# A four-layer transformer pass: residual stream with features on the partitions, norms applied to the finished product tiles

## The reference

```
# first block, for l in 0, 1
x = x + mixer(rms_norm(x, ln_mix[l]))        # w_in, GQA attention and latent attention, 2 output norms, w_o
x = x + memory_attention(rms_norm(x, ln_mem[l]), rms_norm(mem, ln_mem_kv[l]))   # 256 memory rows, 4 heads
x = x + expert_choice_moe(rms_norm(x, ln_ffn[l]))       # 16 experts, 64 tokens each, chosen by top_k
x = rms_norm(x, ln_final)
# second block, for l in 0, 1
x = x + concat(gating, pooling, retention)(rms_norm_2(x, norm1_g[l]) @ w_in[l]) @ w_out[l]
x = x + (silu(conv(h @ w_up)_gate) * conv(h @ w_up)_val) @ w_down[l],  h = rms_norm_2(x, norm2_g[l])
x = rms_norm_2(x, final_g)
# both norms:  x * rsqrt(mean(x * x) + 1e-6) * g     over the 1024 features of a token
```

## Time and profile before

| what | value |
|---|---|
| median of 3 runs | 2554.78 us (2554.11 to 2557.25) |
| the profiled execution: its time | 2554.77 us |
| its span in the profile | 2552.6 us |
| PE, DVE, ACT, POOL busy | 94%, 50%, 36%, 6% |
| mean granted clock of PE | 0.981 of full |
| HBM traffic | 355.76 MB read, 2.10 MB written |

### The profile page before, as it was taken

How to read it: one execution, slowest core, us unless ns; L and a number is a source line. 1 busy time by engine, 2 the same in 40 slices (tenths; PEclk the granted TensorE clock), 3 DMA queues, 4 the chain that set the end, 5 groups by cost and what they waited for, 6 DMA issues and landing times.

```text
span 2552.6 us, 28851 instructions
## 1 busy us (share of the span) xinstructions
PE 2407.1 (94%) x11244; PEld 1717.4 (67%) x11244; DVE 1280.5 (50%) x2170; ACT 920.9 (36%) x1608; POOL 162.6 (6%) x190
## 2 busy tenths in 40 slices
PE   8899996999898999699988999999999999999998
PEld 7655864444575477454446777888887768788887
DVE  4765544333458645523334445666523444666632
ACT  4575542111337745311113224444323213444421
POOL 1301002000021100200001000000000000000000
PEclk9999998999999999899998999999999999999999
DMA  4100406999520023489992212233334212233331
GB/s 176 50 1 34 155 20 255 394 394 394 193 67 17 1 83 124 158 318 394 394 358 92 75 50 83 91 99 99 99 99 133 74 50 76 82 99 99 93 108 56
DMA packets 131830, 359.74 MB, mean 141 GB/s; under 512 B 10992, under 2 KB 12016, under 8 KB 131440
## 3 DMA queue, kind: packets, MB, share of 16 engines
q1 hardware_dynamic: 131408, 357.48, 39.5%
q10 hardware_dynamic: 288, 0.42, 0.1%
HBM read 355.76 MB, written 2.10 MB: 140 GB/s over the span
## 4 chain that ended last, share of the span: by engine, by line
PE 85%; DVE 8%; ACT 4%; POOL 1%; issue 1%; DMA 0%; SPq 0%; POOLq 0%; DVEq 0%; ACTq 0%
PE ps L970 11%; PE ps L972 11%; PE ps L971 11%; PE ps L1188 9%; PE ps L984 6%; PE ps L985 6%; PE ps L986 6%; PE ps L1210 4%; PE ps L1108 3%; PE ps L1081 3%; PE ps L1089 2%; PE ps L1268 1%; PE ps L1150 1%; PE ps L1151 1%; PE ps L958 1%
## 5 line engine op out<-in xcount | busy, mean ns | idle before, releaser
L1855 DVE TENSOR_TENSOR wlo<-stage,whi 128x1024 fp32r<-128x1024 f32 x268 | 327.8, 1226 | 438.1 <-ACT whi L1330 437.6
L970 PE MATMUL ps<-hTh,whi 128*128 128x512 f32 x1232 | 489.8, 398 | 7.7 <-DVE hTl L1814 7.7
L972 PE MATMUL ps<-hTh,wlo 128*128 128x512 f32 x1232 | 480.0, 390 | 0.0
L971 PE MATMUL ps<-hTl,whi 128*128 128x512 f32 x1232 | 479.7, 389 | 0.0
L1330 ACT ACTIVATE whi<-stage 128x1024 fp32r<-128x1024 f32 x268 | 281.3, 1053 | 238.7 <-PE ps L986 238.2
L970 PEld LDWEIGHTS ps<-hTh,whi 128*128 128x128 f32 x1232 | 231.4, 188 | 61.5 <-issue 14.2
L971 PEld LDWEIGHTS ps<-hTl,whi 128*128 128x128 f32 x1232 | 231.5, 188 | 51.0 <-issue 4.3
L972 PEld LDWEIGHTS ps<-hTh,wlo 128*128 128x128 f32 x1232 | 231.3, 188 | 48.9
L1814 DVE SCALAR_TENSOR_TENSOR t<-ps,vecs,t 128x511 f32<-128x511 f32 (+1 forms) x176 | 131.6, 748 | 42.2 <-ACT t L1303 39.1
L1971 DVE TENSOR_REDUCE st<-ps 128x1 f32<-128x512 f32 (+1 forms) x160 | 100.9, 631 | 73.3 <-PE ps L1081 70.2
L984 PE MATMUL ps<-whi,inh 128*128 128x512 f32 x352 | 136.9, 389 | 0.0
(11 more groups left out here) (293 smaller groups left out, 3731.8 us busy)
## 6 DMA issues: line engine op xcount, KB each, us to landing
stage<-in_wpk SPq DMA_DIRECT2D x268, 512.0 KB, 3.6
wt<-in_wg SPq DMA_DIRECT2D x48, 512.0 KB, 11.8
stage<-in_wd SPq DMA_DIRECT2D x48, 512.0 KB, 12.4
ws<-in_wu SPq DMA_DIRECT2D x44, 512.0 KB, 11.5
ws<-in_wg SPq DMA_DIRECT2D x40, 512.0 KB, 11.4
wt<-in_wu SPq DMA_DIRECT2D x40, 512.0 KB, 11.6
wq<-in_wd SPq DMA_DIRECT2D x28, 512.0 KB, 12.5
wt<-in_wd SPq DMA_DIRECT2D x24, 512.0 KB, 12.0
```

The costliest lines, as they stand in the source:

```text
L970: pe.matmul(o, h, ah, start=k == 0, stop=False)
L971: pe.matmul(o, h, al, start=False, stop=False)
L972: t = pe.matmul(o, lo, ah, start=False, stop=k == 7)
L1855: ve.tensor_tensor(M.wlo[i % NW][:, :], M.stage[i % NSTAGE][:, :], f(M.whi[i % NW][:, :]), ALU.subtract).then_inc(*S.wlo.mark(("w", i)))
```

## The change

The residual `x` is held with features on the partitions, [128, 8, 512 tokens], from the first transposes of the input (`x_turn`) to the last stage.

- `om` takes the place of `tm` for the products that add to x (but the last): a chunk's weights are stationary, the activations move, and out is [128 features, 512 tokens] in four banks. As many matmuls of the same size.
- Behind each added tile stands `prep`: ACT copies x times the gain into the stage's `hTh`, then squares x into `nsq`; DVE makes `hTl`; POOL adds the squares to `nacc`. No norm, no `feat` (but for the memory rows).
- `head` takes the first two chunks of mixer, mixer2 and ffn together, k by k (`fmk`), a third behind them; meanwhile `scale` sums `nacc` over the partitions on PE (`nstat`), makes the inverse roots, spreads them over rows (`nrows`) and turns them (`nturn`); ACT copies that to `R`, [128, 512].
- Behind each `fm` of a normed input DVE multiplies the PSUM tile in place by R (`rs`), and what read the tile and waited for PE waits for `rs`.
- `scatter` writes feature tiles. The router stage turns x back into rows by 32 transposes for each layer (`xtok`), scaled by ACT. The final norm of the first block is a product on DVE by its gain and `R0` (`lnf`), and the next stage's statistics take it in through a product on PE (`pstat`).
- The last stage turns x back (`xt`, 32 transposes) and ends as before.
- The parts of mixer2's output (`part`) go to buffers of their own (`y2h`, `y2l`) as soon as these are free, those of the mixers and of the memory attention too.

The core of the diff (layout of buffers, and further waits on `rs` like those shown, are left out):

```diff
-    def fm(self, src, N=512):
+    def fm(self, src, ns, N=512):
         i = self.chunk()
         u = self.take()
         self.do("fm", i, u, src, N)
         self.rel.add(i)
+        if ns is not None:
+            self.do("rs", ns, i, u, 128)
         return i, u
...
+    def om(self, src, K, h, out, before={}):
+        us = [self.take() for _ in range(4)]
+        for c in range(K // 2):
...
+            i = self.chunk()
+            for j in range(4):
...
+                last = c == K // 2 - 1
+                self.do("om", i, us[j], src, c, j, last, j == 3)
+                if last:
+                    out(4 * h + j, us[j], ("om", i, j))
+            self.rel.add(i)
+
+    def residual(self, ns):
+        def go(f, u, key):
+            self.do("add", (ns,), f, u, key)
             self.drop(u)
-            if h == 1 and ahead:
-                self.norm_ahead(ns, m)
+            self.do("prep", ns, f)
         return go
...
+    def scale(self, ns, between=lambda: None):
+        if ns != 6:
+            u = self.take()
+            self.do("nstat", ns, u)
+            self.drop(u)
+        else:
+            self.do("nstat6", self.u6)
+            self.drop(self.u6)
+        self.do("nrows", ns)
+        between()
+        for part in ((0, 1) if ns == 6 else (0,)):
+            u = self.take()
+            self.do("nturn", ns, u, part)
+            self.drop(u)
+
+    def head(self, ns, s):
+        two = [(self.chunk(), self.take()) for _ in range(2)]
+        if ns == 6:
+            self.u6 = self.take()
+        for k in range(8):
+            for i, u in two:
+                self.do("fmk", i, u, s, k)
+            if ns == 6:
+                self.do("pstat", k, self.u6)
+        self.rel |= {two[0][0], two[1][0]}
+
+        def third():
+            two.append(self.fm(s, None))
+        self.scale(ns, third)
+        for i, u in two:
+            self.do("rs", ns, i, u, 128)
+        return two
...
@@ mixer
-        self.feat(s, NT)
+        ready = self.head(ns, s)
...
-        self.tm(("y", l), 8, NT, self.residual(3 * l + 1, 0), {(0, 1): self.tick, 1: self.tick, (1, 2): self.tick, 3: more})
+        self.om(("y", l), 8, 0, self.residual(3 * l + 1), {(0, 1): self.tick, 1: self.tick, (1, 2): self.tick, 3: more})
         self.feat(("memkv", l), 2)
-        self.tm(("y", l), 8, NT, self.residual(3 * l + 1, 1))
+        self.om(("y", l), 8, 1, self.residual(3 * l + 1))
...
@@ mixer2
+        if l == 0:
+            self.do("lnf")
...
@@ ffn
-        self.feat(s, NT)
+        ready = self.head(ns, s)
+
+        def first():
+            return ready.pop(0) if ready else self.fm(s, ns)
         for j in range(22):
-            i, u = self.fm(s)
+            i, u = first()
             self.do("conv", l, j, 0, u, i)
...
+        for m in range(NT):
+            for half in range(2):
+                u = self.take()
+                self.do("xt", m, half, u)
+                self.drop(u)
...
@@ whole
         self.do("start2")
-        for m in range(NT):
-            self.do("norm", 0, m)
+        us = [self.take() for _ in range(8)]
+        self.do("x_turn", us)
+        for f, u in enumerate(us):
+            self.do("x_copy", f, u)
+            self.drop(u)
+            self.do("prep", 0, f)
         for _ in range(2):
             self.do_split()
...
@@ act_program
+        elif name == "prep":
+            ns, k = a
+            src = SRC[ns]
+            q.wait_ge(*S.dve.at("x", ns, k))
+            copy(M.acts[src][k][0], M.x[:, k, :], ("hi", src, k), scale=gain(M, *src, k))
+            if k > 1:
+                q.wait_ge(*(S.pe if ns == 6 else S.pool).at("nacc", ns, k - 2 if ns == 6 else max(k - 2, 1)))
+            copy(M.nsq[k % 2][:, :], M.x[:, k, :], ("nsq", ns, k), f=ACT.Square)
...
@@ act_program, conv (and every other reader of a normed product)
-            q.wait_ge(*S.pe.at("fm", i))
+            q.wait_ge(*S.dve.at("rs", i))
...
@@ dve_program
+        elif name == "prep":
+            ns, k = a
+            src = SRC[ns]
+            hi, lo = M.acts[src][k]
+            q.wait_ge(*S.act.at("hi", src, k))
+            q.wait_ge(*S.dve.at("x", ns, k))
+            stt(lo, M.x[:, k, :], gain(M, *src, k), f(hi), ALU.mult, ALU.subtract, ("lo", src, k))
+        elif name == "rs":
+            ns, i, u, rows = a
+            b = M.ps[u[0]][0:rows, :]
+            q.wait_ge(*S.pe.at("fm", i))
+            q.wait_ge(*S.act.at("R", ns, 0))
+            tt(b, b, M.R[ns][0:rows, :], ALU.mult, ("rs", i))
```

More of the change, by code:

```diff
@@ L650, in mixer2, with last, first @@
             self.drop(u)
-            if n == 5:
-                self.do("point", "hdone2", l)
-                self.hdone = True
-                for p in range(4):
-                    part(p)
-            self.tick()
-        for p in range(4, 8):
-            if self.yf[p] and not self.yt[p]:
-                part(p)
-        self.tm(("y2", l), 8, NT, self.residual(7 + 2 * l, 0), {1: self.tick, 2: self.tick, 3: self.flush})
+            parts()
+            self.tick()
+        parts()
+        def last():
+            self.flush()
+            parts()
+        self.om(("y2", l), 8, 0, self.residual(7 + 2 * l), {1: self.tick, 2: self.tick, 3: last})
         assert not self.later and all(self.yt)
-        self.tm(("y2", l), 8, NT, self.residual(7 + 2 * l, 1))
+        self.om(("y2", l), 8, 1, self.residual(7 + 2 * l))
     def ffn(self, l):
         s = ("ffn", l)
+        ns = 7 + 2 * l
         self.do("point", "ffn", l)
-        self.feat(s, NT)
+        ready = self.head(ns, s)
+        def first():
+            return ready.pop(0) if ready else self.fm(s, ns)
         for j in range(22):
-            i, u = self.fm(s)
+            i, u = first()
             self.do("conv", l, j, 0, u, i)
             self.drop(u)
-            i, u = self.fm(s)
+            i, u = first()
             self.do("conv", l, j, 1, u, i)
@@ L973, in pe_program @@
             t.then_inc(*S.pe.mark(("w", i), ("fm", i)))
+        elif name == "om":
+            i, u, src, c, j, last, lastj = a
+            q.wait_ge(*S.whi.at("w", i))
+            q.wait_ge(*S.wlo.at("w", i))
+            if c == 0:
+                claim(u)
+            o = M.ps[u[0]][:, :]
+            for kk in range(2):
+                r = slice(kk * 512 + 128 * j, kk * 512 + 128 * j + 128)
+                h, lo = M.whi[i % NW][:, r], M.wlo[i % NW][:, r]
+                ah, al = operand(src, 2 * c + kk)
+                pe.matmul(o, h, ah, start=c == 0 and kk == 0, stop=False)
+                pe.matmul(o, lo, ah, start=False, stop=False)
+                t = pe.matmul(o, h, al, start=False, stop=last and kk == 1)
+            if last and lastj:
+                t.then_inc(*S.pe.mark(("om", i, j), ("w", i)))
+            elif last:
+                t.then_inc(*S.pe.mark(("om", i, j)))
+            elif lastj:
+                t.then_inc(*S.pe.mark(("w", i)))
         elif name == "tm":
@@ L1141, in pe_program @@
             t.then_inc(*S.pe.mark(("cum_turn", l)))
+        elif name == "xtok":
+            l, m, half, u = a
+            o = claim(u)
+            for i in range(4):
+                f_ = 4 * half + i
+                q.wait_ge(*S.dve.at("x", 3 * l + 2, f_))
+                t = pe.transpose(o[:, i * 128:(i + 1) * 128], M.x[:, f_, m * 128:(m + 1) * 128], M.ident)
+            t.then_inc(*S.pe.mark(("xtok", l, m, half)))
+        elif name == "xt":
+            m, half, u = a
+            o = claim(u)
+            for i in range(4):
+                q.wait_ge(*S.dve.at("x", 9, 4 * half + i))
+                t = pe.transpose(o[:, i * 128:(i + 1) * 128], M.x[:, 4 * half + i, m * 128:(m + 1) * 128], M.ident)
+            t.then_inc(*S.pe.mark(("xt", m, half)))
         elif name == "gather":
@@ L1428, in act_program @@
             if kind == "mem":
[L1429 to L1430 removed]
+                q.wait_ge(*S.pe.at("point", "memory", l))
+                copy(M.moh[:, p, :], M.ps[u[0]][:, :], ("hi", ("mo", l), p))
                 continue
```

468 lines of the change are left out of this document (283 added, 185 removed).

## The result

The changed kernel takes 2697.3 us (median of 4 runs, 2695.25 to 2699.38), the kernel before 2554.72 on the same chip: a ratio of 1.0556, 95% interval 1.0538 to 1.0574, slower by 142.6 us. The forecast was 2653 with a range of 2612 to 2700: the sign and the main mechanism hold, 44 us of the size don't. The result lies only 2.7 us inside the upper end, and just outside the narrower 2622 to 2696 that the prediction calls its own.

The account below looks back on a forecast made before the run. PE, busy 94% of the span, was taken to bound the kernel. Terms of +91.9, -6.9, -8.3, 0, +6.0 and +16 sum to +98.7 us on the 2554.78 us median: 2653 us, range 2612 to 2700.

Parts of the forecast that it names:

- The ring: Feed-forward: DVE and ACT wait for each other through rs, 13.01 us a step where PE needs 10.88; +91.9 us together.
- Rival A: Feed-forward: rs is hidden, as DVE's busy time with it stays under the span; 2554 us, no change; chance 0.06.
- rival B: Whole kernel: gaps and transposes go, the start hides, nothing new waits; -37.5 us, 2517 us; chance 0.06.
- The sign of what was to be seen: Feed-forward profile: PE waits for DVE wlo of some 43 us in each stage, no other PE wait that large.
- the start: Start of the kernel: prep of all eight tiles stands before the splits 0 and 1; +16 us, first fm at 28.
- the memory stages: Both layers: feat's banks come free later, the new scale chain is 0.8 shorter; +3.4 us each, +2.7 to the router's lgT.
- mixer 1: Mixer of layer 1: some 5 us gained, lost again by stat(cq) behind nturn, 0; a copy 0.7 us later.
- mixer2 of layer 0: Stage after scatter: tiles come 2.05 us apart, both first chunks done at 1354.3 where before 1366.3; -8.3 us.
- rival C: Feed-forward: PE idles 2.1 of 13 us and the granted clock falls; +190 us, 2845 us; chance 0.03.
- leaves 1.0: Feed-forward: the prediction would be wrong if the granted clock there leaves 1.0.
- The step on feat's banks: Memory stages: four banks are freed only by adds that alternate with hTl; second half of om starts 4.2 us later.
- rival D: Start and scatter stages: tiles contend with GpSimd and lose 10 us more; 2663 us; chance within the forecast's 0.82.

Follow-up runs that it names:

- e1: The changed kernel without the product by R in the two feed-forward stages, conv waiting for PE's fm again: 2598.9 us.
- e3: The kernel before, with a DVE product by a tile of ones behind each of the 88 feed-forward fm chunks, conv waiting for it: 2640.6 us.
- e8: The changed kernel with the feed-forward product by R cut to one column, its place in the queue and waits kept: 2650.7 us.
- e4: The changed kernel with the splits of weight chunks 0 and 1 put ahead of x_turn in the list: 2685.6 us.
- e6: The changed kernel with prep of the first four tiles of om(y) put behind feat of the memory rows: 2683.1 us.
- e5: The changed kernel with each add or x_copy put one tile ahead of prep on DVE: 2676.0 us.
- e12: The kernel of e5 with six of GpSimd's seven adds of squares a stage cut to one column: 2671.2 us.

## Why the prediction was right, and where its size failed

**The ring.** Right in place, price and form: 13.05 us for 13.01, 43.1 for 41.2 us in layer 0. rs was taken at 0.68 and has 0.69 (694 ns). The prediction says that no row shows a DVE product written back to PSUM, and puts its range between 422 and 1219 ns. Its rows don't, but the trace of the kernel before does, at the very price:

```profile
L1811 DVE TENSOR_TENSOR ps<-ps,xb 128x512 f32<-128x512 f32 x4 | 2.8, 692 | 0.1
```

e1 removes the ring, e3 brings it into the kernel before, e8 splits it. Rival A (rs hidden under idle time) is what the busy shares suggest, and e3 refutes it by itself; rival B fell with it. The sign of what was to be seen was right, its label not: I expected PE's waits under wlo, 43 us a stage. They stand under "issue", 54.3 us in all: one wait of 1.47 us in a step, of the 2.17 that it loses; the rest of each is drawn as busy matmuls. The number to read was the distance of the steps. The up projection of layer 0 takes 286 us, for 284 forecast.

**The size.** The spans miss the forecast by 46 us, and no error is offset by another: every stretch came out above its figure, the start by 11, the memory stages by 7.7 and 7.2, mixer 1 by 4.1, mixer2 by 7.6 and 2.0, the feed-forward by 1.9 and 3.8. A slip in the sum is small beside this: -12.0 + 2.9 + 1.1 for mixer2 of layer 0 is -8.0, not -8.3.

**The clock (rival C).** In the feed-forward it is 0.99: it lies at the lower level for 3.4 us from 1666.0, behind one wait of 3.24 us for wlo, and is full through all the ring's steps from 1684 to 1918. So C is out there, though by the letter ("leaves 1.0") the prediction's sign of being wrong appeared. Elsewhere the clock falls more: the window of the first products after, and of the first ones before (the earlier trace rows is its first row):

```profile
32.00:48.00 16.00, 15.26 (x61) 12.55 (x62) 3.07 (x4) 3.01 (x4) 0.66 (x1) 0.82 0.29 99
```

```profile
16.00:32.00 16.00, 14.94 (x66) 12.42 (x67) 8.95 (x12) 9.07 (x15) 0.00 (x0) 1.00 0.52 188
```

In the kernel after PE has stood 20 us, and then runs at the lower of its two levels (1.2 GHz) before it goes back to 2.4. The timeline shows it in the distance of the matmuls:

```profile
32.74 0.77 PE L1059 MATMUL ps<-hTh,whi 128*128 128x512 f32 x1 [20.28 <-DVE wlo L2077]
...
36.71 0.63 PE L1059 MATMUL ps<-hTh,whi 128*128 128x512 f32 x1
37.14 0.63 PE L1060 MATMUL ps<-hTh,wlo 128*128 128x512 f32 x1
...
39.31 0.39 PE L1059 MATMUL ps<-hTh,whi 128*128 128x512 f32 x1
39.54 0.39 PE L1060 MATMUL ps<-hTh,wlo 128*128 128x512 f32 x1
```

0.43 us from start to start, then 0.23. For the 512-column matmuls on weight chunks, summed over those that start 0.35 to 0.5 us apart, what they take beyond 0.227 is 3.8 us before and 22.9 after: some 19 of the 46 us, a term that the sum didn't have at all. The lower level is granted from 17.3 to 37.8, where PE stands for the first weights, and in short stretches where PE had waits: at 297.2 between the halves of om(y), at 341.6 and 433.7 behind scale chains, at 737.5 behind the head of mixer 1, at 1392.9 in the head of mixer2.

**The start**, the largest error (+27.8 for +16.7): x_turn's first bank is copied at 11.84 where I put 9.8, an ACT table load of 1.28 us stands before the first hTh, and the tiles come 2.14 us apart, not 2.03: the last hTl is 4.4 us late. The first fm starts at 32.74, 3.4 us behind the 29.3 of the sum. The clock adds 4.7 until the projections' end. The rest of the 11 us isn't split. e4 confirms that the splits behind prep are what makes PE wait, and shows the cure.

**Memory stages** (+10.4 and +9.9 for +2.7 each). The step on feat's banks was right: the second half of om(y) starts 8.5 us behind the end of the first, before 4.1, so 4.4 us later for 4.2 forecast, and e6 takes it out. "The new scale chain is 0.8 shorter" was right too: between the last product of the memory keys and the first of the values lie 3.85 and 3.6 us, before 4.4. What failed is what the sum left out. The key products wait for wlo, whose whi and wlo stand behind the last prep in both queues:

```profile
332.31 0.36 PE L1097 MATMUL ps<-mTh,whi 128*128 128x256 f32 x1 [2.15 <-DVE wlo L2077]
```

Before, the same wait has 0.55: +1.6. The lower clock adds about 4 us in each layer: in layer 0 the second half of om(y) takes 1.4 us more, the values' product 1.1, the end of the attention 1.5, and the granted clock is low in each of them (297.2 to 304.0, 341.6 to 345.0, 396.2 to 399.6), where the kernel before has the full one. And the piece up to the router's lgT costs 0.9 and 0.3 us where a gain of 0.7 was put.

**mixer2 of layer 0** (-1.1 for -8.7): the tiles were to come 2.05 us apart. But ACT's square of tile k waits for PE's pstat of tile k-2, and this stands in PE's queue behind the products of the head. ACT there:

```profile
1396.34 0.63 ACT L1465 ACTIVATE nsq<-x 128x512 f32<-128x512 f32 x1 [1.20 <-PE ps L1070]
...
1400.26 0.63 ACT L1465 ACTIVATE nsq<-x 128x512 f32<-128x512 f32 x1 [2.68 <-PE ps L1070]
```

A second ring, this time through PE at its low clock: the tiles come 2.3 to 2.4 us apart, once 3.9. I counted what the head waits for and not what waits for the head. In mixer 1 (+4.8 for +0.7) the first two chunks are done 3.6 us sooner behind the scatter (19.2 for 22.8), of some 5 that were forecast. Between the third and the fourth chunk PE has 7.4 us in place of 1.5, of which it waits 2.9 for sq ahead of stat(cq) (3.5 were forecast), and the fourth chunk then runs at the lower clock, 8.5 us in place of 5.7. The rest of that term isn't split.

**GpSimd (rival D).** Counted at nothing, and right for this kernel: hTl has 0.75 us in all 72 products, and in this order it and the adds all but take turns: at the start an add runs from 17.48 to 18.74, hTl from 18.96 to 19.71, the next add from 19.53 to 20.84. e5 shows the condition: where DVE no longer waits between tiles, hTl rises to 1113 ns in the mean and the add from 1333 to 1500:

```profile
L1997 DVE SCALAR_TENSOR_TENSOR hTl<-x,vecs,hTh 128x512 fp32r<-128x512 f32 x72 | 79.5, 1113 | 9.7 <-ACT hTh L1472 9.7
L1997 DVE SCALAR_TENSOR_TENSOR hTl<-x,lng,hTh 128x512 fp32r<-128x512 f32 x8 | 6.0, 750 | 5.3 <-ACT hTh L1472 5.3
```

(the second group is mixer2 of layer 0, where PE and not GpSimd sums the squares). On this the Trainium skill, SBUF — State Buffer, section Who interferes with whom, says that a DVE instruction with two SBUF inputs and a GpSimd one that reads SBUF exclude each other. The traces of e5 and e12 agree in direction. In size they show less than exclusion: beside adds an hTl takes 1.10 to 1.28 us in place of 0.75, and 1.75 to 1.79 where it follows another directly (the 1.41 of the expectation is half of a merged row of two, 2.82); the tiles come 1.67 us apart in e5, though hTl and add one behind the other would need 0.75 + 1.33 = 2.08. The 1219 ns by which the prediction judged this, and which it took as an upper bound for rs, are a mean of two kinds in the trace of the kernel before: four of these eight products have 0.75 us with no GpSimd instruction beside them, four have 1.69 beside its `ygl`.

## What to carry to other kernels

Idle time in a queue is no room: before an operation is put on an engine that is busy half the time, write down its queue and that of its partner for one period and follow who waits for whom. If the path comes back to its start within one period, every microsecond on it counts, and so does a mere place in line (52 us here for products of one column). The cure is the order of the list: put what feeds the bottleneck (here the split of the next weights) ahead of what waits for the partner. And where PE will stand or get its tiles one by one, put a term for the lower clock into the sum: here it was 19 us.

## What was not expected of the hardware

- An operation of 159 ns, 88 times (14 us), cost 52 us, most of it by its place.
- The granted clock fell to the 1.2 GHz level at the start, in heads of stages and behind waits, at a cost of some 19 us more than before, while PE gaps of 1.47 us in every 13.05 left it full from 1684 to 1918 us.
- GpSimd's add and DVE's product of two SBUF inputs slow each other where their times overlap: 1.10 to 1.28 us, and 1.75 to 1.79 in a row, in place of 0.75 for DVE, 1.50 in place of 1.33 for GpSimd. They do so by less than if one waited for the whole of the other.
